# Indexer logits in two rounded passes a head, with the attention's first projection chunk between the heads

## The chip, the cores and the metric

The kernel runs on one core of a Trainium2 chip. The metric is the device time of one execution in microseconds. Before the change three runs took 1997.34, 1997.35 and 1994.6 us (median 1997.34).

## The reference

The reference is a stack of four layers on a sequence of 512 tokens with 1024 channels. The change touches the fourth mixer only, a sparse attention whose keys are chosen by an indexer. What it computes for a block of queries is

```python
logits = jnp.einsum('bqhd,bkd->bqhk', qi, k_idx_f)          # 8 index heads, 64 channels, one key for all heads
score = jnp.einsum('bqh,bqhk->bqk', wi, jax.nn.relu(logits))
score = jnp.where(s_pos[None, None, :] <= t_pos[None, :, None], score, -jnp.inf)
_, idx = lax.top_k(score, topk)                             # 128 keys per query
```

`qi`, `ki` and `wi` are columns of one projection of the normed input; other columns of the same projection are the queries, keys and values of the attention. A wrong order of two scores would choose another key, so the logits are wanted in nearly full precision.

## The kernel before

Every matrix product with weights is done in a rounded 32-bit format that TensorE streams faster than plain f32 (its type in the code is `F32R`). To keep precision each operand is split in a high part, which is the operand rounded, and a low part, which is the rest; the product is the sum of three: high by high, high weight by low activation, low weight by high activation (`three`). The activations are the tiles `h_hi` and `h_lo`. The weights come from HBM in chunks of 128x1024 by SyncE, and GpSimd splits them into `w_hi` and `w_lo`, four slots deep; it waits until the chunk four before is used up. A chunk (`tile_chunk`) is eight contraction tiles of three products of 512 columns, 24 products, into one of the four PSUM banks `gemm0` to `gemm3` (`G`). ScalarE copies the result out and so frees the bank.

The order on each engine is written out by hand, and engines wait on semaphores. Around the change it is this. Six chunks (`idx_in`) give the index queries (chunks 0 to 3, two heads of 64 rows each), the index key and the weights `wi` (chunk 4) and the latent rows (chunk 5). ScalarE copies them as plain f32 into tiles of `T2` (`b_t` in the profile); the key is copied twice, to rows 0 to 63 and 64 to 127, since both operands of a product must lie on the same rows. Then `index_logits(h)` runs for eight heads, L938: four products, one for each block of 128 queries, with 128, 256, 384 and 512 keys, as f32 with a contraction over the 64 rows of the head. The record of such a tile reads 64*128. Even heads write banks `G`, odd heads banks `M` (`mix` in the profile). After each head ScalarE evicts three pieces with Relu (L2063 to L2065), and VectorE adds them, weighted, to the score (L1595, L1597), four instructions a head. A head waits until the head two before is evicted. After head 0 four small transposes (L945) turn `wi`.

Behind the heads come eight one-column products for a norm (L953), which wait for the last eviction, then the attention's projection: four chunks, a broadcast of the norm's result (L557), four more chunks, and so on. The tiles go to `G` in the order of the chunks. Meanwhile VectorE takes the 128 largest scores of each query in sixteen rounds, then builds the biases, and meets TensorE again at the attention's logits (L1655).

## Time and profile before

| what | value |
|---|---|
| three runs, median | 1997.34 us |
| the profiled execution, its own time | 1993.52 us |
| its span from first to last instruction | 1991.7 us |
| mean granted TensorE clock | 0.986 |
| TensorE busy | 1926.6 us |
| weight loads | 1554.2 us |
| VectorE / ScalarE / GpSimd busy | 1033.4 / 452.7 / 1185.3 us |

Durations in the profile belong to this one execution. A busy TensorE is not a TensorE at its peak: the record of a product contains the time in the pipeline behind its last column, so that neighbours overlap, and what a product costs in a run is the time from its start to the next start. The granted clock stands as a share of 2.4 GHz: 1.00 is 2.4 GHz and 0.50 is 1.2 GHz. The type f32 is printed for rounded operands too, in the products.

### The profile page before, as it was taken

Reading aid. Unit: us, or ns where it says so; the run is one execution under the profiler, and the core shown is the slowest. Engines: PE = TensorE matmul, PEld = TensorE weight load, DVE = VectorE, ACT = ScalarE, POOL = GpSimd, SP = SyncE. Lnnn points to the kernel's source line nnn. Section 1 sums busy time; section 2 is a strip of 40 time slices with the busy share of each in tenths; the row PEclk is TensorE's granted clock in tenths of the full one; section 3 lists DMA queues with packets and bytes.
Section 4 is the critical chain, followed back from the end, with each engine's and each line's share of the span. In section 5 each row is a group of like instructions: output and inputs, shape, how many; then the busy total and the mean of one; then the engine's idle time right before and its main releaser. Section 6 shows DMA issues by size and latency. Waiting matters only on the chain.

```text
span 1991.7 us, 25332 instructions
## 1 busy us (share of the span) xinstructions
PE 1926.6 (97%) x8824; PEld 1554.2 (78%) x8824; DVE 1033.4 (52%) x1529; ACT 452.7 (23%) x774; POOL 1185.3 (60%) x907
## 2 busy tenths in 40 slices
PE   5999999999999999999999999999998899999998
PEld 4787868888888887667888888886776688888886
DVE  7566256666655453566766663334847453333222
ACT  3302342121110022342211121023118421111100
POOL 3743326788887956325687877743550256666773
PEclk7999999999999999999999999998999999999999
DMA  7532223555555422111455553322220023222332
GB/s 304 178 116 75 95 95 106 182 194 193 190 191 189 159 95 83 61 44 63 159 190 191 188 199 108 109 91 64 85 68 19 24 84 105 95 95 95 105 106 74
DMA packets 67375, 242.23 MB, mean 122 GB/s; under 512 B 7498, under 2 KB 7882, under 8 KB 67314
## 3 DMA queue, kind: packets, MB, share of 16 engines
q1 hardware_dynamic: 65536, 237.01, 34.4%
q10 hardware_dynamic: 1778, 4.37, 0.6%
q8 instruction: 43, 0.70, 0.2%
q14 instruction: 18, 0.15, 0.0%
HBM read 239.25 MB, written 2.10 MB: 121 GB/s over the span
## 4 chain that ended last, share of the span: by engine, by line
PE 89%; DVE 4%; ACT 3%; issue 2%; DMA 2%; POOL 1%; SPq 0%; ACTq 0%; DVEq 0%; POOLq 0%
PE gemm L446 24%; PE gemm L447 23%; PE gemm L448 23%; PE gemm L473 2%; PE gemm L475 2%; PE gemm L474 2%; DMA w_raw<-wstream 2%; PE mix L649 1%; PE gemm L802 1%; PE mix L446 1%; PE gemm L1036 1%; DVE sq_acc L1355 1%; PE mix L447 1%; PE mix L448 1%; PE gemm L816 1%
## 5 line engine op out<-in xcount | busy, mean ns | idle before, releaser
L430 POOL TENSOR_TENSOR w_lo<-w_raw,w_hi 128x1024 fp32r<-128x1024 f32 x302 | 735.7, 2436 | 25.2
L446 PE MATMUL gemm<-h_hi,w_hi 128*128 128x512 f32 x1616 | 634.4, 393 | 21.7 <-DVE h_lo L1176 14.9
L447 PE MATMUL gemm<-h_lo,w_hi 128*128 128x512 f32 x1616 | 631.0, 390 | 0.0
L448 PE MATMUL gemm<-h_hi,w_lo 128*128 128x512 f32 x1616 | 630.9, 390 | 0.0
L427 POOL TENSOR_TENSOR pool_gate<-pool_gate 128x1 f32<-128x1 f32 x298 | 118.3, 397 | 736.0 <-PE gemm L448 596.1
L446 PEld LDWEIGHTS gemm<-h_hi,w_hi 128*128 128x128 f32 x1616 | 304.7, 189 | 90.7 <-issue 22.6
L448 PEld LDWEIGHTS gemm<-h_hi,w_lo 128*128 128x128 f32 x1616 | 304.6, 188 | 63.8
L428 POOL TENSOR_SCALAR w_hi<-w_raw 128x1024 fp32r<-128x1024 f32 x302 | 344.2, 1140 | 16.9 <-DMA w_raw<-wstream 16.9
L447 PEld LDWEIGHTS gemm<-h_lo,w_hi 128*128 128x128 f32 x1616 | 304.7, 189 | 62.4
L1070 DVE CUSTOM_DVE_ANT_0 ada_raw<-ada_raw,c_act 128x1024 f32<-128x1024 f32 x128 | 218.3, 1722 | 108.4 <-DMA ada_raw<-adastream 108.4
L448 PE MATMUL gemm<-p_hi,w_lo 128*128 128x512 f32 x528 | 205.4, 389 | 0.0
L446 PE MATMUL gemm<-p_hi,w_hi 128*128 128x512 f32 x528 | 205.4, 389 | 0.0
L447 PE MATMUL gemm<-p_lo,w_hi 128*128 128x512 f32 x528 | 205.4, 389 | 0.0
L1088 DVE SCALAR_TENSOR_TENSOR x_res<-gemm,modv,x_res 128x512 f32<-128x512 f32 x48 | 35.9, 748 | 239.5 <-PE gemm L448 239.5
L1383 DVE TENSOR_TENSOR work<-work,gemm 128x512 f32<-128x512 f32 x66 | 45.4, 688 | 176.5 <-PE gemm L448 138.7
L1385 DVE TENSOR_TENSOR p_lo<-work,p_hi 128x512 f32 x66 | 97.5, 1477 | 61.4 <-ACT p_hi L1917 61.4
L1714 ACT ACTIVATE sq_tile<-x_res 128x512 f32 x48 | 30.4, 633 | 430.3 <-DVE x_res L1088 430.3
L1355 DVE TENSOR_TENSOR sq_acc<-sq_acc,sq_tile 128x512 f32<-128x512 f32 x42 | 98.8, 2353 | 36.7 <-ACT sq_tile L1714 36.7
L448 PEld LDWEIGHTS gemm<-p_hi,w_lo 128*128 128x128 f32 x528 | 99.1, 188 | 20.8
L446 PEld LDWEIGHTS gemm<-p_hi,w_hi 128*128 128x128 f32 x528 | 99.1, 188 | 20.6
L447 PEld LDWEIGHTS gemm<-p_lo,w_hi 128*128 128x128 f32 x528 | 99.1, 188 | 20.4
L1911 ACT ACTIVATE work<-work 128x512 f32<-128x512 f32 x44 | 27.9, 634 | 307.9 <-DVE work L1378 307.9
(341 smaller groups left out, 1970.4 us busy)
## 6 DMA issues: line engine op xcount, KB each, us to landing
w_raw<-wstream SPq DMA_DIRECT2D x302, 512.0 KB, 3.5
ada_raw<-adastream SPq DMA_DIRECT2D x128, 512.0 KB, 4.3
a_early<-adastream SPq DMA_DIRECT2D x8, 1024.0 KB, 11.8
out<-x_res SPq DMA_DIRECT2D x8, 256.0 KB, 2.2
c_act<-c_in ACTq DMA_DIRECT2D x2, 512.0 KB, 7.2
x_res<-x_in SPq DMA_DIRECT2D x2, 512.0 KB, 6.2
x_res<-x_in ACTq DMA_DIRECT2D x2, 512.0 KB, 9.1
b_dist<-const_in ACTq DMA_DIRECT2D x1, 512.0 KB
```

Of the source, the lines that this page charges most:

```text
L427: pool.tensor_tensor(pgate[:], pgate[:], pgate[:], ALU.mult)
L428: pool.tensor_scalar(whi[s][:], raw[:, u % RAW, :], 1.0, 0.0, ALU.mult, ALU.add).then_inc(w_hi_done, 1)
L430: pool.tensor_tensor(wlo[s][:], raw[:, u % RAW, :], whi[s][:].bitcast(F32), ALU.subtract).then_inc(w_split, 1)
L446: pe.matmul(out_ap, w_h, r_h, start=first, stop=False)
L447: pe.matmul(out_ap, w_h, r_l, start=False, stop=False)
L448: return pe.matmul(out_ap, w_l, r_h, start=False, stop=last)
L473: pe.matmul(G[j][:], a, wh, start=(k == 0), stop=False)
L474: pe.matmul(G[j][:], a, wl, start=False, stop=False)
L1070: dve.tensor_tensor_reduce(w, w, c, 1.0, start, ALU.mult, ALU.add, total).then_inc(ada_used, 1)
L1355: dve.tensor_tensor(sqacc[:], sqacc[:], sqt[:, m % 2, :], ALU.add).then_inc(sq_added, 1)
L1383: dve.tensor_tensor(work[:, 2 + jj, :], y, G[2 * jj + 1][:], ALU.mult).then_inc(gfree[2 * jj + 1], 1)
L1385: dve.tensor_tensor(Plo[:, ds(2 * i + jj, 1), :].rearrange("p a t -> p (a t)"), work[:, 2 + jj, :], Phi[:, ds(2 * i + jj, 1), :].rearrange ...
```

## The change

ScalarE now copies each index query tile five times: once as plain f32, and for each of its two heads the rounded value to rows 0 to 63 and to rows 64 to 127 of a tile of its own (`T2R`, the same memory as `T2` under the rounded type, `b_t_hilo` in the profile). VectorE subtracts the rounded value from the plain one, which gives the low part of the queries. The key tile `IDX_K2` gets the high part on rows 0 to 63 and the low part on rows 64 to 127, the tile `IDX_KD` the high part on both.

A block of logits is then two products in the rounded format. The first contracts over 128 rows: the high query, twice, against high and low key. The second contracts over the 64 rows of the head: the low query against the high key. The products of high by high, high by low and low by high are the same three as elsewhere.

The first chunk of the attention's projection no longer stands behind the norm's products. Its eight contraction tiles are done in pieces: two after head 1, and one after each of heads 2 to 7. It uses bank `G[3]`, which the heads don't use; the banks of the chunks behind it turn by one.

```diff
--- before.py
+++ after.py
@@ -288,6 +288,7 @@
             Z = [zmem[:, TRI * i:TRI * i + TRI] for i in range(3)] + [cact[:].rearrange("p m n -> p (m n)")[:, 0:TRI]]
             PS = sb("b_pt", [P, 2, TRI], F32, r)
             VB = work
+            IDX_Q, IDX_K2, IDX_KD = 6, 14, 15
             SB5 = M + [G[3]]
             rows = sqacc
             wuk = sb("b_wuk", [P, 4, P], F32, r)
@@ -301,6 +302,9 @@
             sm = sb("b_sm", [P, 16], F32, r)
 
 
+        with ExitStack() as r:
+            sb("r_over_h", [P, 2 * KT * T], F32, r)
+            T2R = sb("b_t2_hilo", [P, 18, T], F32R, r)
         const_in_sem = sem("const_loaded")
         x_loaded = [sem(f"x_loaded{m}") for m in range(4)]
         cols_loaded = sem("cols_loaded")
@@ -927,40 +931,60 @@
                 if h == 0:
                     for u in range(4):
                         pe.wait_ge(gfree[u], G0["attn_in"][u])
+                    pe.wait_ge(sig("ixk_low"), 1)
                 if h == 1:
                     pe.wait_ge(sig("wi_ready"), 1)
                     pe.wait_ge(sig("x_normed"), KT)
                 if h >= 2:
 
                     pe.wait_ge(sig("ix_relu"), h - 1)
+                pe.wait_ge(sig("ixq_low"), h + 1)
                 for j in range(NTB):
                     b, o = BANK_J[j]
-                    mm = pe.matmul(bk[b][:, o:o + P * (j + 1)], T2[rows, h // 2, j * P:(j + 1) * P], T2[rows, 4, 0:P * (j + 1)],
-                                   start=True, stop=True)
+                    n = P * (j + 1)
+                    pe.matmul(bk[b][:, o:o + n], T2R[:, IDX_Q + h, j * P:(j + 1) * P], T2R[:, IDX_K2, 0:n], start=True, stop=False)
+                    mm = pe.matmul(bk[b][:, o:o + n], T2R[rows, h // 2, j * P:(j + 1) * P], T2R[rows, IDX_KD, 0:n],
+                                   start=False, stop=True)
                 mm.then_inc(sig("ix_mm"), 1)
+
+            def first_query_chunk(ks):
+
+                n = N0["attn_in"]
+                s = n % SPL
+                for k in ks:
+                    if k == 0:
+                        pe.wait_ge(w_split, n + 1)
+                    mm = three(G[3][:], whi[s][:, k * P:(k + 1) * P], wlo[s][:, k * P:(k + 1) * P],
+                               Hhi[:, k, :], Hlo[:, k, :], k == 0, k == KT - 1)
+                if ks[-1] == KT - 1:
+                    mm.then_inc(pe_done, 1)
 
             index_logits(0)
 
             for j in range(NTB):
                 mm = pe.transpose(M[3][:, 8 * j:8 * j + 8], wirow[:, j * P:(j + 1) * P], const("ident")[0:8, 0:8])
             mm.then_inc(sig("wi_t"), 1)
-            for h in range(1, 8):
+            index_logits(1)
+            first_query_chunk((0, 1))
+            for h in range(2, 8):
                 index_logits(h)
+                first_query_chunk((h,))
 
             pe.wait_ge(sig("ckv_sq"), 1)
             pe.wait_ge(sig("ix_relu"), 8)
             for j in range(NTB):
                 mm = pe.matmul(normps[:, j:j + 1], sqt[:, 0, j * P:(j + 1) * P], const("ones")[:, 0:1], start=True, stop=True)
             mm.then_inc(norm_sum, 1)
-            def attn_tiles(first):
-
-                for u in range(4):
-                    tile_chunk(N0["attn_in"] + first + u, (N0["attn_in"] + u) % SPL, u, G0["attn_in"][u] + first // 4)
-
-            attn_tiles(0)
+            def attn_tiles(chunks):
+
+                for c in chunks:
+                    bank = (c + 3) % 4
+                    tile_chunk(N0["attn_in"] + c, (N0["attn_in"] + c) % SPL, bank, G0["attn_in"][bank] + c // 4)
+
+            attn_tiles(range(1, 4))
             bc[0] += 1
             bcast(rstdps, bc[0])
-            attn_tiles(4)
+            attn_tiles(range(4, 8))
 
             pe.wait_ge(sig("ckv_n"), 1)
             for u in range(4):
@@ -1576,7 +1600,19 @@
             ffn("ffn1", 1, COL["fconv_w"] + 66, 25, 21, C2, 11)
             down("down1", 4, 88, gain=True)
             norm(7, 6, col("g_attn", 0, 8), (96, 104), first_gain=col("final_g", 0, 8))
+            def index_lows(c):
+
+                for e in range(2):
+                    r = slice(64 * e, 64 * e + 64)
+                    dve.wait_ge(sig("ixq_high"), 2 * c + e + 1)
+                    dve.tensor_tensor(T2R[r, c, :], T2[r, c, :], T2R[r, IDX_Q + 2 * c + e, :].bitcast(F32),
+                                      ALU.subtract).then_inc(sig("ixq_low"), 1)
+
             normed_x(4, col("final_g", 0, 8), bank=M[1], done=True)
+            for c in range(4):
+                index_lows(c)
+            dve.wait_ge(sig("ixk_high"), 1)
+            dve.tensor_tensor(T2R[64:128, IDX_K2, :], T2[0:64, 4, :], T2R[0:64, IDX_K2, :].bitcast(F32), ALU.subtract).then_inc(sig("ixk_low"), 1)
 
             dve.wait_ge(small_loaded, 96)
 
@@ -2048,10 +2084,18 @@
                 if c == 4:
 
                     act.activation(T2[0:64, 4, :], G[0][0:64, :], ACT.Copy)
-                    act.activation(T2[64:128, 4, :], G[0][0:64, :], ACT.Copy)
+                    act.activation(T2R[0:64, IDX_K2, :], G[0][0:64, :], ACT.Copy).then_inc(sig("ixk_high"), 1)
+                    act.activation(T2R[0:64, IDX_KD, :], G[0][0:64, :], ACT.Copy)
+                    act.activation(T2R[64:128, IDX_KD, :], G[0][0:64, :], ACT.Copy)
                     act.activation(wirow, G[0][64:72, :], ACT.Copy, scale=IDX_SCALE).then_inc(gfree[0], 1)
+                elif c == 5:
+                    act.activation(T2[:, c, :], G[c % 4][:], ACT.Copy).then_inc(gfree[c % 4], 1)
                 else:
-                    act.activation(T2[:, c, :], G[c % 4][:], ACT.Copy).then_inc(gfree[c % 4], 1)
+                    act.activation(T2[:, c, :], G[c][:], ACT.Copy)
+                    act.activation(T2R[64:128, IDX_Q + 2 * c, :], G[c][0:64, :], ACT.Copy)
+                    act.activation(T2R[0:64, IDX_Q + 2 * c, :], G[c][0:64, :], ACT.Copy).then_inc(sig("ixq_high"), 1)
+                    act.activation(T2R[64:128, IDX_Q + 2 * c + 1, :], G[c][64:128, :], ACT.Copy).then_inc(sig("ixq_high"), 1)
+                    act.activation(T2R[0:64, IDX_Q + 2 * c + 1, :], G[c][64:128, :], ACT.Copy).then_inc(gfree[c], 1)
             act.activation(rms[:, 30:31], cols[:, 0:1], ACT.Copy).then_inc(sig("ckv_sq"), 1)
             act.wait_ge(sig("wi_t"), 1)
             act.activation(wi[:], M[3][:, 0:32], ACT.Copy).then_inc(sig("wi_ready"), 1)
@@ -2072,9 +2116,9 @@
                 act.activation(T2[:, tile, :], G[bank][:], ACT.Copy, scale=scale).then_inc(gfree[bank], 1)
 
             for u in range(4):
-                evict(u, u, 10 + u, 0.125)
+                evict(u, (u + 3) % 4, 10 + u, 0.125)
             for u in range(4):
-                evict(4 + u, u, 14 + u)
+                evict(4 + u, (u + 3) % 4, 14 + u)
             for u in range(4):
                 act.wait_ge(sig("kb_mm"), u + 1)
                 act.activation(T2[:, u, :], M[u][:], ACT.Copy).then_inc(sig("kb_copied"), 1)
```

TensorE, from the last product of the projection `idx_in` through head 0 and the transposes to the start of head 1. Before (`b_t` are the index tiles in f32; `gemm` and `mix` are the PSUM banks):

```order
L448 MATMUL gemm<-h_hi,w_lo 128x512
L938 MATMUL gemm<-b_t 128x128
L938 MATMUL gemm<-b_t 128x256
L938 MATMUL gemm<-b_t 128x384
L938 MATMUL gemm<-b_t 128x512
L945 MATMUL mix<-cst,b_pt 128x8 x4
L938 MATMUL mix<-b_t 128x128
```

After, in the same place, and on to the end of head 1, its six products of the chunk and the start of head 2 (L945 is now the product over 128 rows, L946 the one over 64):

```order
L945 MATMUL gemm<-b_t_hilo 128x384
L946 MATMUL gemm<-b_t_hilo 128x384
L945 MATMUL gemm<-b_t_hilo 128x512
L946 MATMUL gemm<-b_t_hilo 128x512
L965 MATMUL mix<-cst,b_pt 128x8 x4
L945 MATMUL mix<-b_t_hilo 128x128
L946 MATMUL mix<-b_t_hilo 128x128
```

```order
L945 MATMUL mix<-b_t_hilo 128x512
L946 MATMUL mix<-b_t_hilo 128x512
L450 MATMUL gemm<-h_hi,w_hi 128x512
L451 MATMUL gemm<-h_lo,w_hi 128x512
L452 MATMUL gemm<-h_hi,w_lo 128x512
L450 MATMUL gemm<-h_hi,w_hi 128x512
L451 MATMUL gemm<-h_lo,w_hi 128x512
L452 MATMUL gemm<-h_hi,w_lo 128x512
L945 MATMUL gemm<-b_t_hilo 128x128
L946 MATMUL gemm<-b_t_hilo 128x128
L945 MATMUL gemm<-b_t_hilo 128x256
```

Products over 128 and over 64 rows take turns within a head, and full products stand between heads.

ScalarE, the copies of the six projection chunks. Before:

```order
L2054 ACTIVATE b_t<-gemm 128x512 x4
L2050 ACTIVATE b_t<-gemm 64x512
L2051 ACTIVATE b_t<-gemm 64x512
L2052 ACTIVATE b_pt<-gemm 8x512
L2047 ACTIVATE sq_tile<-gemm 128x512
L2054 ACTIVATE b_t<-gemm 128x512
```

After, the fourth query tile, the key and the latent rows:

```order
L2097 ACTIVATE b_t_hilo<-gemm 64x512
L2098 ACTIVATE b_t_hilo<-gemm 64x512
L2086 ACTIVATE b_t<-gemm 64x512
L2087 ACTIVATE b_t_hilo<-gemm 64x512
L2088 ACTIVATE b_t_hilo<-gemm 64x512
L2089 ACTIVATE b_t_hilo<-gemm 64x512
L2090 ACTIVATE b_pt<-gemm 8x512
L2083 ACTIVATE sq_tile<-gemm 128x512
L2092 ACTIVATE b_t<-gemm 128x512
```

One copy of a query tile became five, and three of the key's chunk became five.

## Rows read from the trace of the kernel before

**Rows 1.** The page's header and TensorE's share of the span.
```profile
span 1991.7 us, 25332 instructions
PE 1926.6 (97%) x8824; PEld 1554.2 (78%) x8824; DVE 1033.4 (52%) x1529; ACT 452.7 (23%) x774; POOL 1185.3 (60%) x907
```

**Rows 2.** The chain of waits, 1330 to 1480 us: start, duration, what.
```profile
1364.96 1.36 issue
1366.33 2.39 PE gemm L938 x8
...
1385.11 0.60 ACT ada_raw L2063
...
1386.62 1.81 PE mix L953 x8
```

**Rows 3.** Time line of TensorE: start, duration, tile, shapes, count, idle before.
```profile
1368.65 0.41 PE L945 MATMUL mix<-cst,b_pt 8*128 8x8 f32 x4
1369.35 2.10 PE L938 MATMUL mix<-b_t 64*128 64x128 f32 x5 [0.29 <-ACT b_wi L2057]
...
1388.30 0.77 PE L446 MATMUL gemm<-h_hi,w_hi 128*128 128x512 f32 x1
...
1394.24 0.39 PE L446 MATMUL gemm<-h_hi,w_hi 128*128 128x512 f32 x1
...
1396.28 0.39 PE L446 MATMUL gemm<-h_hi,w_hi 128*128 128x512 f32 x1
```

**Rows 4.** Stretches: length, busy time (count) of each engine, clock, DMA share, GB/s.
```profile
1369.60:1372.90 3.30, 3.30 (x14) 2.76 (x14) 1.27 (x4) 0.95 (x3) 0.00 (x0) 0.50 0.49 159
1373.00:1386.60 13.60, 11.16 (x44) 6.35 (x43) 11.19 (x24) 9.43 (x21) 0.00 (x0) 1.00 0.00 0
1386.70:1393.40 6.70, 6.70 (x20) 5.64 (x21) 6.33 (x20) 0.27 (x1) 0.00 (x0) 0.50 0.00 0
1393.50:1412.00 18.50, 18.50 (x83) 15.29 (x82) 16.13 (x51) 1.80 (x3) 10.86 (x9) 1.00 0.17 57
```

**Rows 5.** Time line of TensorE: 40-row products between 128-row ones, clock 1.00.
```profile
822.02 0.50 PE L789 MATMUL mix<-o_gm_hilo,o_sel 40*128 40x512 f32 x1
822.45 0.50 PE L446 MATMUL mix<-h_hi,w_hi 128*128 128x512 f32 x1
...
914.75 0.40 PE L448 MATMUL gemm<-h_hi,w_lo 128*128 128x512 f32 x1
915.08 0.96 PE L850 MATMUL mix<-o_gm_hilo,o_sel 40*128 40x512 f32 x3
915.97 0.50 PE L446 MATMUL gemm<-h_hi,w_hi 128*128 128x512 f32 x1
916.31 0.39 PE L447 MATMUL gemm<-h_lo,w_hi 128*128 128x512 f32 x1
```

**Rows 6.** The same where the clock is 0.50.
```profile
807.79 0.79 PE L789 MATMUL mix<-o_gm_hilo,o_sel 40*128 40x512 f32 x1
808.51 0.79 PE L446 MATMUL mix<-h_hi,w_hi 128*128 128x512 f32 x1
809.10 0.63 PE L447 MATMUL mix<-h_lo,w_hi 128*128 128x512 f32 x1
```

**Rows 7.** Time line of ScalarE, copies of the index projection.
```profile
1348.68 0.60 ACT L2054 ACTIVATE b_t<-gemm 128x512 f32<-128x512 f32 x1 [5.77 <-PE gemm L448]
...
1365.00 0.60 ACT L2047 ACTIVATE sq_tile<-gemm 128x512 f32<-128x512 f32 x1 [3.64 <-PE gemm L448]
```

**Rows 8.** Time line of VectorE, scores and the start of the attention.
```profile
1370.68 1.27 DVE L1595 TENSOR_SCALAR b_score<-ada_raw,b_wi 128x128 f32<-128x128 f32 x4 [22.12 <-ACT ada_raw L2065]
1374.89 14.19 DVE L1597 SCALAR_TENSOR_TENSOR b_score<-ada_raw,b_wi,b_score 128x128 f32<-128x128 f32 x28 [2.93 <-ACT ada_raw L2065]
...
1413.69 0.69 DVE L1626 TENSOR_TENSOR b_t<-b_t,mix 128x512 f32<-128x512 f32 x1 [1.96 <-PE mix L557]
...
1468.76 0.29 DVE L1655 CUSTOM_DVE_ANT_0 ada_raw<-mix,b_bias 128x128 f32<-128x128 f32 x1 [9.38 <-PE mix L987]
```

## The prediction, on record before the result

> **What bounds the kernel now.** I first read the page's header and busy shares [rows 1]: TensorE is busy for 1926.6 of 1991.7 us. The chain of waits over the stretch of the change [rows 2] then shows what sets the end there. It runs almost wholly over TensorE: an idle 1.36 us (two evictions of the last projection chunk on ScalarE), the index logits, the evictions of the last head, eight one-column products, and the first chunk of the attention's projection. The time line of TensorE [rows 3] gives the stations: the heads begin at 1366.33, the one-column products at 1386.62, the first attention chunk at 1388.30, the second at 1396.28. So 29.95 us pass from the first logit to the second chunk, and the change has to be judged by what becomes of this stretch. The table of stretches [rows 4] adds the clock: 0.50 (1.2 GHz instead of 2.4) at 1369.6 to 1372.9 and again at 1386.7 to 1393.4. Last come the rows that show what a pass costs when its neighbours use another number of array rows [rows 5, 6].
>
> **The logits, passes alone.** A rounded 512-column product follows the next after 0.227 us (nine of them from 1394.24 to 1396.28 [rows 3]), one column a cycle at 2.4 GHz plus 0.014. A head has 128 + 256 + 384 + 512 = 1280 columns. In f32 they are the eight records of 1366.33, and the next instruction starts 2.32 us later [rows 2, 3]: four cycles a column, 2.13, and a tail. After there are two rounded passes a block: 2 x 1280 / 2400 = 1.07 us. Eight heads would win 8.5 us.
>
> **What the two passes add.** One pass contracts over 128 rows, the other over 64, and they alternate: eight changes of row count in a head (the order in the section on the change shows it). The trace has such changes of rounded products. One 40-row product of 512 columns between products of 128 rows: 822.02 to 822.45, so 0.43 us from start to start against the 0.23 of a run of equal ones [rows 5]. A run of three such products shows the parts: 0.33 into it (914.75 to 915.08), three of them until 915.97, and 0.34 instead of 0.23 from the first to the second after it. So the stop costs about 0.10 before the change and 0.11 for weights that are no longer loaded ahead: 0.21 on top of the stream for a pass that stands alone between two changes. The two head terms are then 8 x 0.21 + 1.07 = 2.75 us at 2.4 GHz: more than the 2.32 of before. At 1.2 GHz the 40-row product took 0.72 (807.79 to 808.51) and the second product behind it starts 0.59 after the first, where a run of equals has 0.43 [rows 6]: 0.29 a pass, so 2.13 + 8 x 0.29 = 4.5 us a head. The small blocks have no such row; I give them the same 0.21. Their bounds: nothing added (the second rival) and 0.21; I take 0.21, since the change came out the same wherever the trace has it.
> The Trainium skill (TensorEngine Tiling, section Key Properties) states that changing the tiling mode, unlike changing the tile within a mode, drains TensorE; by that rule, the trace agrees, with the 0.10 us above.
>
> **The chunk between the heads.** It moves 24 rounded products of 512 columns, 24 x 0.227 = 5.4 us, from behind the heads to between them. Before it took 7.98 us (1388.30 to 1396.28), because its first products ran at the low clock [rows 3, 4]: 2.5 us are lost there. A piece of three costs 0.68, plus 0.11 for its second weight load; the next head's first pass saves its 0.10.
>
> **The sum at the full clock.** Head 0: 1366.33 + 2.75 = 1369.1. Transposes and the copy of the weights, unchanged: 0.70 (1368.65 to 1369.35) [rows 3], so 1369.8. Head 1: 1372.5. Six products: 1.47, 1374.0. Six periods of 2.75 - 0.10 + 0.68 + 0.11 = 3.44: 1394.6. The one-column products wait for the evictions of head 7 (its passes end at 1393.8, evictions from 1385.11 to 1386.62 with the hand-over, 1.5 [rows 2]: 1395.3) and took 1.68 at the low clock (1386.62 to 1388.30 [rows 2, 3]), so 0.85 here: chunk two at 1396.2, against 1396.28. The passes' gain is spent on the changes, and the hidden chunk's on the longer heads. Nothing is left at this clock.
>
> **The clock.** It decides. It was down by 1369.6 in the trace: what stood before was the 1.36 us stop, 2.3 us of 64-row passes and the small transposes [rows 2 to 4]. It fell again behind the last head, with the 1.54 us wait. It came back by 1393.5, after five microseconds of full products without a gap (from 1388.30), and stayed [rows 4]. In the new kernel the first heads stand at the same place, behind the same stop, around the same transposes, and they stream 1.07 us in 2.75, half of it on 64 rows. So I expect the fall there too. The difference comes afterwards. Before, the next two heads' 64-row passes filled 1369.6 to 1372.9 without a gap (3.30 of 3.30 us busy), and the clock is back at 1373 [rows 4]. After, every head is stop and go, and between two heads stand only three products: 1.3 us, nothing like the unbroken run that brought the clock back. I let the loop run at 1.2 GHz to its end. Head 1: 1369.8 + 4.5 = 1374.3. Six products at 0.427 and one bare load of 0.17: 1377.0. Six periods of 4.5 + 1.28 = 5.8 (a load of 0.17 saved and one paid): 1411.7. Head 7 ends at 1410.4, evictions until 1411.9, the one-column products 1.7 (1386.62 to 1388.30, at this clock): 1413.6. The next chunk pays the way back to 2.4 GHz: before it was the 2.5 us; I take 1.9, since heads and pieces before it keep the engine busier than a wait did. That is 1415.5 against 1396.28: **+19.2 us**.
>
> **What hides the rest.** ScalarE gets 18 more activations (16 for four query tiles, two for the key), 0.60 us each. Eight of them follow the first two tiles, 4.8 us, where it then idles 5.77; two follow the key, 1.2 us, where it idles 3.64 [rows 7]. So 2.4 us of cover stand ahead of the last eviction, which frees the bank that head 0 waits for; what exceeded them would be added to the start. VectorE gets nine subtractions, and is idle for 22.12 us before the scores [rows 8], 2.5 us for each; the last one waits for the key's copy only, some four microseconds before head 0. The split weights of the attention's fifth chunk still wait for the end of its first, with three chunks (16 us) between them, so POOL's split and SP's transfer move along. VectorE's scores are 14.19 us for seven heads, 2.03 a head [rows 8], under the period of 3.44 or 5.8. But the last sum is now late: about 1413.9 instead of 1389.08, +24.9. The attention's first projection tiles arrive +19.2. VectorE has 9.38 us idle before the attention logits and 1.96 before the row of the norm, which goes since TensorE comes by one chunk earlier [rows 8]. 9.38 + 1.96 - 24.9 + 19.2 = 5.6 us are left, so VectorE does not set the end.
>
> **The time.** The profiled run took 1993.52, the three timed ones 1994.6 to 1997.35 with a median of 1997.34; their mean over all four is 1995.7. With +19.2 this gives 2014.9, told as 2015. By the profile alone it would be 2012.7, by the median 2016.5.
>
> **Rivals.**
> First, the clock holds, or comes back behind head 1 where six products stand together (2.6 us, with the wide passes around them). For it: the stretch 1373 to 1386.6 had waits of its own, 11.16 of 13.60 us busy, and held 1.00 [rows 4]; the pieces add full rows. Against it: head 0 and 1. It gives -0.1 if it never falls. If it falls for head 1 and the six, add 1.75 and 1.3, some +3 to +4. 1995.6 to 1999.7.
> Second, faster: the changes of row count cost nothing, since loads and drains overlap when both passes belong to one block. Then a head is 8 passes, 1.07 + 8 x 0.014 = 1.2 us, with its piece 1.9, and VectorE's 2.03 a head becomes the pace: head 1 ends at 1369.4, the six products at 1370.8, six times 2.03 to 1383.0, evictions and one-column products until 1385.3: -11 us, 1984.7. It decides once a pass costs less than 0.15 over its stream: 64 passes, 0.06 less each, are 4 us. For it: the small blocks and changes inside one block stand in no row. Against it: every change in rows 5 and 6 costs 0.2 and more.
> Third, the copies on ScalarE delay the start: at most a microsecond or two, by the cover above.
>
> **Chances.** Forecast 0.60, clock holds or returns 0.25, faster 0.13, worse than the forecast 0.02. A measurement of this kernel tells 0.2%, 4 us, from no change. So faster 0.13, same 0.25, slower 0.62. The range goes from the lower end of the first rival by the profiled run (1993.4) to the median plus 19.2 and a chunk wholly at the low clock (some +4): 1993 to 2020. The likeliest case alone: 2011 to 2019.
>
> **What would show it.** In the new profile: the 128-row and 64-row logit passes start 0.21 us apart beyond their stream (a 512-column pass 0.43); the clock reads 0.50 from about 1369 to 1415; the stretch from the first logit to the attention's second chunk is 49 us instead of 30; VectorE waits for ScalarE in the scores; its idle time before the attention logits shrinks to under 6 us. The forecast is wrong if the clock is 1.00 in the loop (then no change), or if passes follow each other at stream length (then faster).

## The result, and the profile after

The changed kernel is a little slower. Its median over 16 runs is 1998.88 us, against 1994.74 us over the same number of runs of the kernel before on the same chip (1990.49 to 1997.56): +4.1 us. The ratio is 1.0052, with a 95% interval of 1.0030 to 1.0073. It lies further above 1 than the two medians do (1.0021), since the 16 runs fall into two groups: nine at 1996.4 to 1999.1 us with a mean granted clock of 0.985 to 0.988, and seven at 2014.0 to 2018.5 us with 0.973 to 0.976. The profiled run, 2015.76 us, is of the upper group. All three profiles of this kernel are, so the rows here show that group alone.

The page's header and busy shares, as [rows 1]:
```profile
span 2014.0 us, 25365 instructions
PE 1950.7 (97%) x8824; PEld 1564.9 (78%) x8824; DVE 1050.0 (52%) x1538; ACT 462.8 (23%) x792; POOL 1186.1 (59%) x907
```
TensorE has exactly as many instructions as before, 8824: each head's four f32 products had two records each, and now it has eight rounded passes. It is busy for 24.1 us more.

The time line of TensorE, as [rows 3]: head 0 at the full clock, head 4 at the half clock, and the end of the loop.
```profile
1367.90 0.30 PE L945 MATMUL gemm<-b_t_hilo 128*128 128x128 f32 x1 [1.36 <-issue]
1368.13 0.32 PE L946 MATMUL gemm<-b_t_hilo 64*128 64x128 f32 x1
...
1369.76 0.50 PE L945 MATMUL gemm<-b_t_hilo 128*128 128x512 f32 x1
1370.19 0.50 PE L946 MATMUL gemm<-b_t_hilo 64*128 64x512 f32 x1
1370.62 0.41 PE L965 MATMUL mix<-cst,b_pt 8*128 8x8 f32 x4
...
1390.12 0.31 PE L945 MATMUL gemm<-b_t_hilo 128*128 128x128 f32 x1
...
1394.46 0.79 PE L450 MATMUL gemm<-h_hi,w_hi 128*128 128x512 f32 x1
...
1413.43 1.84 PE L976 MATMUL mix<-cst,sq_tile 128*128 128x1 f32 x8
1415.13 0.77 PE L450 MATMUL gemm<-h_hi,w_hi 128*128 128x512 f32 x1
...
1418.69 0.41 PE L452 MATMUL gemm<-h_hi,w_lo 128*128 128x512 f32 x1
```
Head 0 takes 1367.90 to 1370.62, 2.72 us; its 512-column passes stand 0.43 apart. A head at the half clock takes 1390.12 to 1394.46, 4.34 us (0.17 of a weight load stand in the piece around it). The second chunk starts at 1415.13, 47.2 us after the first logit, against 29.95 us before [rows 3].

The stretch of the loop, as [rows 4]: busy time (count) of TensorE, weight loads, VectorE, ScalarE, GpSimd, then the granted clock, the DMA share, GB/s.
```profile
1371.00:1418.60 47.60, 47.31 (x97) 27.59 (x97) 18.15 (x35) 11.74 (x27) 3.98 (x3) 0.50 0.03 11
```
The half clock covers 47.6 us without a break. Before, it covered twice, 3.3 and 6.7 us [rows 4].

The chain of waits (start, duration, what), as [rows 2]:
```profile
1382.96 0.72 PE gemm L450
...
1388.74 0.72 PE gemm L450
```
It stays on TensorE throughout; between the pieces L450, one behind each head, lie 5.78 us. The one-column products L976 no longer wait for ScalarE.

The time line of ScalarE, as [rows 7]:
```profile
1350.26 0.60 ACT L2094 ACTIVATE b_t<-gemm 128x512 f32<-128x512 f32 x1 [0.94 <-PE gemm L452]
...
1366.58 0.60 ACT L2083 ACTIVATE sq_tile<-gemm 128x512 f32<-128x512 f32 x1 [2.68 <-PE gemm L452]
```
That of VectorE, as [rows 8]:
```profile
1350.06 12.95 DVE L1608 TENSOR_TENSOR b_t_hilo<-b_t,b_t_hilo 64x512 fp32r<-64x512 f32 x8
1363.04 2.77 DVE L1615 TENSOR_TENSOR b_t_hilo<-b_t,b_t_hilo 64x512 fp32r<-64x512 f32 x1
...
1491.12 0.29 DVE L1691 CUSTOM_DVE_ANT_0 ada_raw<-mix,b_bias 128x128 f32<-128x128 f32 x1 [4.06 <-PE mix L1011]
```
ScalarE still idles 0.94 us after the first two tiles and 2.68 us after the key's copies. VectorE's nine subtractions end at 1365.8, two microseconds ahead of head 0. Before the attention logits VectorE idles 4.06 us, where it had 9.38.

Some of VectorE's instructions are longer than their equals. VectorE and GpSimd in two places of the same trace, the subtractions and the last head's sums:
```profile
1355.59 0.69 DVE L1608 TENSOR_TENSOR b_t_hilo<-b_t,b_t_hilo 64x512 fp32r<-64x512 f32 x1
...
1361.42 1.05 POOL L432 TENSOR_SCALAR w_hi<-w_raw 128x1024 fp32r<-128x1024 f32 x1
1361.43 1.57 DVE L1608 TENSOR_TENSOR b_t_hilo<-b_t,b_t_hilo 64x512 fp32r<-64x512 f32 x1
1362.55 2.71 POOL L434 TENSOR_TENSOR w_lo<-w_raw,w_hi 128x1024 fp32r<-128x1024 f32 x1
...
1413.70 1.27 POOL L432 TENSOR_SCALAR w_hi<-w_raw 128x1024 fp32r<-128x1024 f32 x1
1413.99 4.17 DVE L1633 SCALAR_TENSOR_TENSOR b_score<-ada_raw,b_wi,b_score 128x384 f32<-128x384 f32 x2
1415.06 2.56 POOL L434 TENSOR_TENSOR w_lo<-w_raw,w_hi 128x1024 fp32r<-128x1024 f32 x1
```
A subtraction takes 0.69 us with no split beside it, 1.57 beside GpSimd's L432 and 2.77 beside its L434, whose end (1365.26) it outlasts by half a microsecond. The last two sums, L1633, take 4.17 us for two, where before they took 1.27:
```profile
1387.81 1.27 DVE L1597 SCALAR_TENSOR_TENSOR b_score<-ada_raw,b_wi,b_score 128x384 f32<-128x384 f32 x2
```
Since the first attention chunk is now used up right behind head 7, GpSimd's next split starts at 1413.70 and falls on them; before, it started at 1396.68, 7.6 us behind their end.

The spans differ by 22.3 us. From head 0 to the first product of the attention's scores (at 1487.00 after and 1466.33 before; VectorE's L1691 waits for these products) 119.1 us pass instead of 100.0: +19.1. Head 0 starts 1.57 us later, since the clock fell once more early in that run (about 3.4 us at 190 us), and another short fall of the clock, at 1487.0, makes these products some 1.6 us longer.

### The profile page after: what moved, and what is told of

Same layout as the page of the kernel before. It is cut to its first block, busy times and chain, and to the rows that moved or that the text cites. A ratio compares the mean times of both kernels' runs of the same rounds, so it can differ in the third digit from the quotient of the medians.

```text
span 2014.0 us, 25365 instructions
## 1 busy us (share of the span) xinstructions
PE 1950.7 (97%) x8824; PEld 1564.9 (78%) x8824; DVE 1050.0 (52%) x1538; ACT 462.8 (23%) x792; POOL 1186.1 (59%) x907
## 4 chain that ended last, share of the span: by engine, by line
PE 89%; DVE 4%; ACT 3%; issue 2%; DMA 1%; POOL 1%; SPq 0%; ACTq 0%; DVEq 0%; POOLq 0%
PE gemm L450 23%; PE gemm L452 23%; PE gemm L451 23%; PE gemm L477 2%; PE gemm L479 2%; PE gemm L478 2%; DMA w_raw<-wstream 1%; PE mix L653 1%; PE gemm L806 1%; PE mix L450 1%; DVE sq_acc L1379 1%; PE gemm L1060 1%; PE mix L452 1%; PE mix L451 1%; PE gemm L820 1%
## 5 line engine op out<-in xcount | busy, mean ns | idle before, releaser
L434 POOL TENSOR_TENSOR w_lo<-w_raw,w_hi 128x1024 fp32r<-128x1024 f32 x302 | 735.7, 2436 | 25.2
L450 PE MATMUL gemm<-h_hi,w_hi 128*128 128x512 f32 x1616 | 637.0, 394 | 21.7 <-DVE h_lo L1200 14.9
L450 PEld LDWEIGHTS gemm<-h_hi,w_hi 128*128 128x128 f32 x1616 | 305.2, 189 | 93.3 <-issue 25.3
L432 POOL TENSOR_SCALAR w_hi<-w_raw 128x1024 fp32r<-128x1024 f32 x302 | 344.8, 1142 | 16.9 <-DMA w_raw<-wstream 16.9
L450 PE MATMUL gemm<-p_hi,w_hi 128*128 128x512 f32 x528 | 205.4, 389 | 0.0
L450 PEld LDWEIGHTS gemm<-p_hi,w_hi 128*128 128x128 f32 x528 | 99.1, 188 | 20.7
L451 PEld LDWEIGHTS gemm<-p_lo,w_hi 128*128 128x128 f32 x528 | 99.1, 188 | 20.5
L452 PEld LDWEIGHTS gemm<-p_hi,w_lo 128*128 128x128 f32 x528 | 99.1, 188 | 20.5
```

The source lines that it names most:

```text
L432: pool.tensor_scalar(whi[s][:], raw[:, u % RAW, :], 1.0, 0.0, ALU.mult, ALU.add).then_inc(w_hi_done, 1)
L434: pool.tensor_tensor(wlo[s][:], raw[:, u % RAW, :], whi[s][:].bitcast(F32), ALU.subtract).then_inc(w_split, 1)
L450: pe.matmul(out_ap, w_h, r_h, start=first, stop=False)
L451: pe.matmul(out_ap, w_h, r_l, start=False, stop=False)
L452: return pe.matmul(out_ap, w_l, r_h, start=False, stop=last)
```

## The experiments

Four theories stood against each other. A: a change between 128 and 64 rows costs 0.21 us, as in the prediction. B: every short pass costs that, whatever its neighbours. C: VectorE or ScalarE already sets the pace. D: the two groups are two courses of the clock, and it comes back, where it does, in the unbroken full products behind head 1. Kernels are compared with the kernel before on the same chip; "low" is the stretch at clock 0.50. The times in this table are from head 0's start to the start of the next whole chunk and to the first product of the attention's scores, each in one profile:

| kernel | low in the loop | to the next chunk | to the attention's scores |
|---|---|---|---|
| before | 3.4 and 6.8 us | 21.97 | 100.0 |
| the change | 47.8 us | 47.23 | 119.1 |
| grouped passes | 6.8 us | 24.22 | 94.4 |
| padded low pass | 3.4 us | 19.98 | 90.1 |
| logits only | 37.6 us | 37.99 | 115.2 |
| chunk only | 51.2 us | 49.01 | 121.5 |
| run of nine | 51.2 us | 48.51 | 121.4 |
| run of nine, second profile | 10.2 and 6.8 us | 35.51 | 107.9 |
| one piece each | 47.8 us | 46.65 | 118.9 |
| filled stops | none | 18.84 | 89.0 |

The next chunk is the attention's first in "before" and "logits only", its second in the others.

**Grouped passes.** The eight passes of a head are ordered so that the row count changes twice, not eight times. All products are the same.
```diff
-                for j in range(NTB):
+                wide = [(True, j) for j in (1, 2, 3)]
+                for full, j in wide + [(False, j) for j in (1, 2, 3, 0)] + [(True, 0)]:
```


> The changed kernel with the passes of a head in another order: wide passes of blocks 1, 2, 3, then the 64-row passes of 1, 2, 3, 0, then the wide pass of block 0. Two changes of row count in a head instead of eight, the same passes. Theory A (every change of row count costs a stop of 0.10 us and a bare weight load of 0.11): a head takes 1.07 + 0.11 + 2 x 0.21 = 1.6 us instead of 2.75, the period with its piece 2.3; about 9 us faster than before at the full clock, about 5 slower than before where the clock stays at 1.2 GHz through the loop, and that should be rarer than in the changed kernel, since the engine streams more of the time. Theory B (each short rounded pass costs 0.2 over its stream whatever stands beside it, because a 128-column weight load isn't hidden): a head still takes 2.75 us, and the time is that of the changed kernel.

Measured: 1989.20 us (1987.30 to 1991.28, six runs) against 1996.03; ratio 0.9966 (0.9954 to 0.9978), −6.8 us. Time line of TensorE:
```profile
1378.88 1.72 PE L948 MATMUL mix<-b_t_hilo 128*128 128x256 f32 x8
1380.43 0.45 PE L450 MATMUL gemm<-h_hi,w_hi 128*128 128x512 f32 x1
...
1381.19 1.72 PE L948 MATMUL gemm<-b_t_hilo 128*128 128x256 f32 x8
```
Its low stretch:
```profile
1371.10:1377.90 6.80, 6.80 (x19) 4.97 (x18) 3.22 (x8) 1.92 (x5) 0.00 (x0) 0.50 0.24 77
```
A head is 1.55 us (1378.88 to 1380.43) and the period 2.31. Against the 2.72 us of head 0 in the change, six changes fewer save 1.17, 0.20 each; against the 2.62 us of a head inside the loop (the run of nine, below) 1.07, 0.18 each. A holds. B, by which the order would change nothing, falls. The clock falls here too, behind the same stop, but it comes back after 6.8 us, behind the six products and near the end of head 2. All six runs lie within 4 us: no second group.

**Padded low pass.** The low query is multiplied over 128 rows as well. The second key tile exists twice, each with zeros on the rows of the other head, so that the product is the same and no row count changes.
```diff
-                    mm = pe.matmul(bk[b][:, o:o + n], T2R[rows, h // 2, j * P:(j + 1) * P], T2R[rows, IDX_KD, 0:n],
+                    mm = pe.matmul(bk[b][:, o:o + n], T2R[:, h // 2, j * P:(j + 1) * P], T2R[:, IDX_KD + h % 2, 0:n],
...
-                    act.activation(T2R[64:128, IDX_KD, :], G[0][0:64, :], ACT.Copy)
+                    act.activation(T2R[64:128, IDX_KD + 1, :], G[0][0:64, :], ACT.Copy)
+                    act.activation(T2R[64:128, IDX_KD, :], G[0][0:64, :], ACT.Copy, scale=0.0)
+                    act.activation(T2R[0:64, IDX_KD + 1, :], G[0][0:64, :], ACT.Copy, scale=0.0)
```


> The low-query pass also over 128 rows: the low parts of both heads of a tile against a key tile that holds the high key on the head's 64 rows and zeros on the other 64 (two such tiles, so two more copies on ScalarE). No change of row count anywhere in the loop but at the transposes. Theory A: a head takes 1.07 + 8 x 0.014 = 1.2 us, the period 1.9, and VectorE's 2.03 us a head becomes the pace; 11 us faster than before. Clock at 2.4 GHz behind head 1, since full rows stream nearly all the time. Theory B: as the changed kernel, 2.75 us a head. Theory C (VectorE or ScalarE pace the loop already): no gain over the changed kernel either, with TensorE idle between heads.

Measured: 1983.59 us (1982.41 to 1985.14, six runs); ratio 0.9939 (0.9927 to 0.9951), −12.4 us. No version of the study is faster. The time line of TensorE:
```profile
1371.78 0.22 PE L945 MATMUL gemm<-b_t_hilo 128*128 128x128 f32 x1
...
1372.59 0.39 PE L945 MATMUL gemm<-b_t_hilo 128*128 128x512 f32 x1
1372.82 0.40 PE L946 MATMUL gemm<-b_t_hilo 128*128 128x512 f32 x1
1373.06 0.40 PE L450 MATMUL gemm<-h_hi,w_hi 128*128 128x512 f32 x1
...
1373.75 0.22 PE L945 MATMUL mix<-b_t_hilo 128*128 128x128 f32 x1
...
1384.60 1.02 PE L976 MATMUL mix<-cst,sq_tile 128*128 128x1 f32 x8 [0.85 <-ACT ada_raw L2111]
```
The only stretch of its loop in which the clock is low:
```profile
1367.30:1370.60 3.30, 3.01 (x11) 2.68 (x11) 1.27 (x4) 1.66 (x5) 0.58 (x1) 0.50 0.44 135
```
Passes of 512 columns follow at 0.23 us, a head is 1.28 us and the period 1.97. As many passes, as short as in the change, now cost little more than their stream of 1.07 us: the price was the change of rows. C falls too, for the change: the period shrinks to 1.97 with VectorE's work as it was and two copies more on ScalarE. VectorE doesn't set this period, as the expectation had it: its last six heads take 14.97 us from 1374.65, 2.5 us each, and end 4.1 us behind the start of the next chunk (1385.48), and no eviction waits for them. The clock is low for 3.4 us.

**Logits only.** The two-pass logits of the change, with the attention's first chunk where it was before, behind the norm's products, and the banks in the old turn.
```diff
-            index_logits(1)
-            first_query_chunk((0, 1))
-            for h in range(2, 8):
+            for h in range(1, 8):
                 index_logits(h)
-                first_query_chunk((h,))
...
-            attn_tiles(range(1, 4))
+            attn_tiles(0)
```


> The two passes of logits, with the attention's first chunk where it was before, behind the heads. Theory A: 2.75 us a head at 2.4 GHz, so the second chunk starts 0.6 us later than in the kernel before, at 1.2 GHz 4.5 us a head and some 16 us later. Without full products between the heads the low clock should be the rule here: 14 to 18 us slower than before in most runs. Rival (it is the pieces between the heads that lose the time): no slower than before.

Measured: 2010.04 us (2009.45 to 2013.54, six runs); ratio 1.0076 (1.0063 to 1.0089), +14.0 us. The low stretch in the table of stretches:
```profile
1369.80:1407.20 37.40, 35.86 (x71) 19.81 (x71) 17.39 (x42) 10.51 (x24) 0.00 (x0) 0.50 0.03 13
```
With nothing but such heads the clock stays at 0.50 to their end and 3.4 us into the chunk behind them (which starts at 1365.89 + 37.99). All six runs have a mean clock of 0.977 to 0.980, so none came back early.

**Chunk only.** The f32 logits of before, without the copies and subtractions; only the chunk moves between the heads.
```diff
-                    n = P * (j + 1)
-                    pe.matmul(bk[b][:, o:o + n], T2R[:, IDX_Q + h, j * P:(j + 1) * P], T2R[:, IDX_K2, 0:n], start=True, stop=False)
-                    mm = pe.matmul(bk[b][:, o:o + n], T2R[rows, h // 2, j * P:(j + 1) * P], T2R[rows, IDX_KD, 0:n],
-                                   start=False, stop=True)
+                    mm = pe.matmul(bk[b][:, o:o + P * (j + 1)], T2[rows, h // 2, j * P:(j + 1) * P], T2[rows, 4, 0:P * (j + 1)],
+                                   start=True, stop=True)
```


> The f32 logits of before, with the attention's first chunk in pieces between the heads. Theory A: a head streams 2.13 us, two changes of row count and the piece bring the period to 3.1; 3 us faster than before if the clock holds at 2.4 GHz. If the clock falls in the loop as in the profiled run of the changed kernel, a period is about 6 us and the time 15 us over that of before. Rival (the chunk's first products at the low clock were the whole gain to be had, and it comes without the rounded logits): 2.5 us or more faster in every run.

Measured: 2016.49 us (2014.39 to 2021.13, five runs); ratio 1.0101 (1.0087 to 1.0115), +20.5 us. Time line of TensorE, head 1 and what follows:
```profile
1373.83 4.63 PE L938 MATMUL mix<-b_t 64*128 64x128 f32 x8 [0.29 <-ACT b_wi L2073]
1378.39 0.79 PE L446 MATMUL gemm<-h_hi,w_hi 128*128 128x512 f32 x1
```
The low stretch:
```profile
1373.60:1424.70 51.10, 50.87 (x100) 28.14 (x101) 19.36 (x39) 11.72 (x27) 3.98 (x3) 0.50 0.06 16
```
This one I had wrong on its cause. TensorE is busy for 50.87 of 51.10 us, the row count changes only twice a period, and yet the clock stays low in the profile, and by the mean clocks (0.973 to 0.977) in every run. So eight changes of row count a head, or TensorE standing still, are not needed for it to stay low. In the kernel before, the same f32 heads stand in the trace at clock 1.00 as well as at 0.50 [rows 4]. One thing that the pieces take from them can be seen there. Time line of TensorE before, heads 3 (`mix`) and 4 (`gemm`) and the start of head 5:
```profile
1374.91 1.56 PE L938 MATMUL mix<-b_t 64*128 64x128 f32 x6 [0.72 <-ACT ada_raw L2065]
1376.16 0.37 PE L938 MATMUL gemm<-b_t 64*128 64x128 f32 x1
...
1376.74 0.59 PE L938 MATMUL mix<-b_t 64*128 64x512 f32 x1
...
1378.78 1.99 PE L938 MATMUL mix<-b_t 64*128 64x128 f32 x7 [0.20 <-ACT ada_raw L2065]
```
Two f32 heads on different halves of the rows interleave: head 4 begins at 1376.16 while products of head 3 still come until 1376.74, and the two pass in 3.87 us, a wait of 0.20 included, where head 0 alone takes 2.32. With three full products between them each head stands alone, 4.56 us at the half clock. That is part of the loss; why the clock stays down is not explained. It also says that neither half of the change is good alone: +14.0 and +20.5, together +4 or +20.

**Run of nine.** For theory D: three pieces behind head 1 instead of two, then one after each of heads 2 to 6 and none behind head 7.
```diff
-            first_query_chunk((0, 1))
+            first_query_chunk((0, 1, 2))
             for h in range(2, 8):
                 index_logits(h)
-                first_query_chunk((h,))
+                if h < 7:
+                    first_query_chunk((h + 1,))
```


> The changed kernel with its pieces of the attention's first chunk placed otherwise: three contraction tiles (nine products) after head 1, one after each of heads 2 to 6, none after head 7. All instructions are the same. Theory D (the two groups of times of the changed kernel, about 1998 and about 2016, are two courses of the clock in the loop, and it comes back where a long enough run of full products stands behind head 1): the unbroken run at the low clock grows from 2.6 to 3.9 us, the clock comes back there in every run, and all runs lie near the lower group, 3 to 5 us over the kernel before. Rival (the two groups have another cause, for example the weights' transfers, or the place of the run plays no part): again two groups, or all in the upper one.

Measured: 2004.59 us in the median of six runs, ratio 1.0042 (1.0028 to 1.0055). The profiled one took 2016.26 at clock 0.975, the others 2002.39 to 2005.65 at 0.982 to 0.984. By these times and clocks five came back and one did not; and those that did cost +7 to +10 us, not the +3 to +5 expected. A second profile of it was taken:

> The kernel with nine products after head 1 and none after head 7, looked at once more, since its profile is of its one slow run (2016.26) and five others lie at 2002 to 2006. Theory D: in such a run the clock is back behind the nine products, and what it is above the lower group of the changed kernel (4 to 7 us) comes from the end of the loop: with no piece after head 7 TensorE waits 0.7 us longer for its evictions, and the clock falls there as it did in the kernel before, 2.5 us. Rival: the clock comes back later, behind another head.

It took 2007.58 us, and shows the course with the return. Time line of TensorE:
```profile
1386.67 0.22 PE L945 MATMUL mix<-b_t_hilo 128*128 128x128 f32 x1
...
1389.29 0.50 PE L450 MATMUL gemm<-h_hi,w_hi 128*128 128x512 f32 x1
...
1390.09 0.22 PE L945 MATMUL gemm<-b_t_hilo 128*128 128x128 f32 x1
...
1404.65 1.84 PE L977 MATMUL mix<-cst,sq_tile 128*128 128x1 f32 x8 [1.54 <-ACT ada_raw L2110]
```
The stretches:
```profile
1373.60:1383.70 10.10, 9.81 (x25) 6.28 (x24) 3.21 (x8) 2.81 (x7) 0.00 (x0) 0.50 0.15 52
1383.80:1404.20 20.40, 19.31 (x61) 10.77 (x61) 10.85 (x18) 7.87 (x18) 3.46 (x3) 1.00 0.00 0
1404.30:1411.00 6.70, 6.35 (x19) 5.41 (x20) 6.33 (x19) 0.96 (x3) 0.00 (x0) 0.50 0.24 81
```
The nine products run from 1378.94 to 1382.94 and the clock is 1.00 from 1383.76. From there a head is 2.62 us and the period 3.42 (1386.67 to 1390.09), the period that the prediction gave for the full clock. The second low stretch accounts for 3.4 us of what such a run costs: without a piece behind head 7 TensorE waits 1.54 us before the one-column products, as before [rows 2], and the clock falls again, for 6.8 us. In the profile that stayed low the same nine products stand from 1374.05 to 1378.06, 4.9 us behind the fall instead of 5.4, and the clock stays at 0.50 through them and until 1420.35:
```profile
1369.20:1420.30 51.10, 49.27 (x102) 29.40 (x102) 22.23 (x48) 11.74 (x27) 3.96 (x3) 0.50 0.07 21
```
The instructions up to the fall are the same in both, but the fall comes 3.0 us behind the start of head 0 here (1366.14), as in the three profiles of the change, and 2.7 us behind it (1370.84) in the profile with the return. Whether that decides the course, one profile with a return can't tell.

**One piece each.** The other way: piece 0 behind the transposes, before head 1, and one behind each of heads 1 to 7, so that nowhere more than three products stand together.
```diff
-            index_logits(1)
-            first_query_chunk((0, 1))
-            for h in range(2, 8):
+            first_query_chunk((0,))
+            for h in range(1, 8):
```


> The changed kernel with one contraction tile after each of the eight heads, so that no run longer than three products stands in the loop. The first stands behind the transposes, in TensorE's wait before head 1. Theory D: once the clock is down it has nowhere to come back; all runs, or nearly all, in the upper group, 18 to 20 us over the kernel before, unless the piece in the wait keeps it from falling at all. Rival (run length plays no part): two groups in the same shares as in the changed kernel, 0.7 us earlier.

Measured: 2015.10 us (2013.75 to 2018.03, four runs), ratio 1.0103 (1.0087 to 1.0118). The low stretch:
```profile
1369.40:1417.10 47.70, 47.70 (x98) 27.64 (x97) 18.90 (x38) 11.54 (x26) 3.98 (x3) 0.50 0.05 14
```
No run came back: all four are in the upper group, with mean clocks of 0.974 to 0.976, though the piece before head 1 leaves TensorE no stop in the low stretch. With the later profiles the change stays out of the upper group in nine of 18 runs, and the run of nine in six of seven. So the clock was spared or returned in none of four, nine of 18 and six of seven runs, in the order of the run's length. That fits D as a matter of frequency, not as the rule that I had expected. It is not proven: the runs are few, the change can't be told apart from either neighbour by them, the two versions also differ in what stands before head 1 and behind head 7, and a return is seen in one profile alone.

**The change again.** Two more profiles of the changed kernel, to catch one of its lower group.

> The changed kernel itself, looked at once more, since its one profile is of the upper group of its times (2015.76). Theory D: a run of the lower group (near 1998) has the clock back at 2.4 GHz right behind the six products of head 1, or not lost in the loop at all; the periods of heads 2 to 7 are then 3.44 us, head 2 begins about 3 us later than at the full clock, and the second chunk begins 3 to 4 us later from head 0 than before. A run of the upper group repeats the first profile.

> As the look before: one more chance for a profile of the lower group, with the same expectations.

2015.69 and 2014.04 us: both in the upper group again, with the low stretch as long to a tenth (47.8 us). There is no profile of the lower group.

**Filled stops.** The padded version, with pieces where TensorE stood still: two in the stop before head 0, one behind the transposes, none behind heads 1 and 7.
```diff
+            pe.wait_ge(gfree[3], G0["attn_in"][3])
+            first_query_chunk((0, 1))
             index_logits(0)
...
+            first_query_chunk((2,))
             for h in range(1, 8):
```


> The kernel with the padded key tiles (no change of row count in the loop), with two contraction tiles of the attention's chunk in the 1.36 us stop before head 0, one in the wait behind the transposes, none after head 1, and one after each of heads 2 to 6. The loop is paced by VectorE at 2.03 us a head from head 1 on, and starts it at the same point; head 2 comes 1.4 us earlier and head 7's evictions about 1 us earlier: 1 to 1.5 us faster than the padded kernel, and the clock doesn't fall at head 0 any more, 0.5 us more. Rival (the loop's end is set by TensorE's own work, which is only moved): 2 us faster, the length of the stops filled. Rival (the chain is that of ScalarE and VectorE alone): the same time as the padded kernel.

Measured: 1985.89 us (1983.24 to 1987.29, five runs), ratio 0.9952 (0.9938 to 0.9965). Time line of TensorE:
```profile
1367.77 0.30 PE L945 MATMUL gemm<-b_t_hilo 128*128 128x128 f32 x1
...
1385.73 1.02 PE L979 MATMUL mix<-cst,sq_tile 128*128 128x1 f32 x8 [2.80 <-ACT ada_raw L2114]
```
ScalarE's waits for VectorE in the loop (us in total, times, longest):
```profile
ACT ada_raw L2112 <- DVE b_score L1636: 4.3, 5, 1.5
```
The stretch in which all its heads lie:
```profile
1366.00:1390.00 24.00, 21.19 (x117) 17.90 (x116) 17.42 (x32) 12.95 (x30) 8.10 (x6) 1.00 0.21 66
```
In this profile the clock never falls in the loop. So the fall of the padded version, 3.4 us, hangs on the stops around the first heads, 1.36 us before head 0 and 0.29 before head 1, which are filled here. The second alone is not it: the one piece each fills that one too, and its clock falls. For the kernels with changes of row count the filled stops were not tried. But the stop comes back at the end: TensorE waits 2.80 us for the last evictions, where the padded version waits 0.85. The evictions of heads 3 to 7 wait for VectorE's sums, 4.3 us together, so here VectorE does set the pace, as expected. From head 0 to the next chunk it gains 1.14 us, in the total nothing that can be told: 9.2 us under its own runs of before, 12.4 for the padded version.

## Why the prediction was right and where it was wrong

The sign was right, and the measured median lies in the range. The forecast of 2015 us was right for seven runs of 16, wrong for the median. That the range holds it is owed to the first rival, from which its lower end comes; the likeliest case alone, 2011 to 2019, misses it. And +4.1 us is not a size that the mechanism gave: it depends on how many of the 16 runs fell in each group.

**What failed is a step of the part on the clock: "I let the loop run at 1.2 GHz to its end."** I took this as the course of every run and gave it 0.60. In nine of 16 runs the mean clock is about 0.986, not 0.975. What that means can be checked in size: at 0.975 of 2014 us the lost share is 2 x 0.025 x 2014 = 101 us at the half clock; at 0.986 of 1996 it is 56 us. The 45 us between them are nearly the low stretch of 47.8 us. So in these runs the clock is not low through the loop, and at +1.6 to +4.4 us over the median of before they are my first rival (+3 to +4, chance 0.25). Whether it comes back early or doesn't fall there at all the mean clocks can't tell: a step of 0.001 in them is 4 us at the half clock. That it comes back at the six products is inferred: from the run of nine, where a trace shows it behind nine, and from the one piece each, where no run returned. Which of the two courses a run takes is open. The instructions are the same; the two profiles of the run of nine differ ahead of their nine products in the moment of the fall (3.0 and 2.7 us behind the start of head 0), and two profiles don't settle it.

**The terms, where the clock was as forecast.** A head at the full clock: 2.75 us told, 2.72 and 2.62 measured. A period at the full clock 3.44, measured 3.42; at the half clock 5.8, measured 5.78. From first logit to the end of the one-column products 47.3 us (1413.6 less 1366.33), measured 47.23; the 49 us among the signs are the same with the way back to the full clock added. The way back, told as 1.9: the next chunk's first eight products take 3.56 us from start to start (1415.13 to 1418.69), where eight at 0.227 are 1.8, so 1.7. Head 0 to the attention's scores: +19.2 told, +19.1 measured.

**The change of row count.** 0.21 us for each lone pass was taken from 40-row products [rows 5]. On 64 rows it is 0.43 from start to start for 512 columns, 0.23 for 128 (0.053 streamed), so 0.18 to 0.22: the small blocks, which stood in no row, cost the same. Grouping and padding show that it is the change of row count that costs, and not the length of a pass. The second rival (changes cost nothing, −11 us) named what the kernel would be without it: 1.2 us a head, 2 us a period. The padded version is that kernel, 1.28 and 1.97, −12.4 us. What the f32 heads cost was read too high: 2.32 us is a head alone, and at the full clock two of them pass in 3.87 us (heads 3 and 4, shown with the chunk only), 1.94 each. So the passes had no 8.5 us to win on heads of 2.13 us and a tail. The sum was not hurt by it, since it was held against the measured end of the loop.

**What hides the rest.** ScalarE's cover of 2.4 us held: its idle time of 5.77 before the third tile shrank to 0.94, by the 4.8 told, and that of 3.64 to 2.68. VectorE's subtractions were under 2.5 us on average, as allowed (12.95 us for eight), but more than twice the 0.69 us of one with no split beside it, and the last one ended 2.1 us before head 0, not four. The slack before the attention logits was 4.06 us instead of 5.6. There the prediction let GpSimd's split "move along" and did not look at what it moves onto: the last head's sums, which became 2.9 us longer (4.17 less 1.27). The sums ended 50.3 us behind the first logit, and 47.6 were told. The other 1.2 us, which came the other way, I did not separate. None of it reached the end, since the slack covered it. The Trainium skill (SBUF — State Buffer, section "SBUF: two separate sides") states that VectorE and GpSimd arbitrate for one pair of ports, which one instruction holds for its whole length while the other waits, where VectorE's instruction has two inputs in SBUF. The trace agrees: 0.69 us with no split beside it, and beside one 1.57 and 2.77 us, ending about half a microsecond behind the split each time.

## What to carry to other kernels

A rounded product is priced by its start-to-start distance beside the neighbours that it will have: two short passes with another row count each can cost more than the f32 product that they replace, above all where f32 products on different halves of the rows interleave. Zero rows that keep the count the same, or passes grouped by row count, took this from +4 to −12.4 and −6.8 us. Where a stretch begins behind a stop of TensorE, work out both courses of the clock, give neither all the weight, and time enough runs to see whether there are two groups.

## What the runs showed of the hardware

- The same program took two courses of the clock on one chip, with medians 18 us apart, nine to seven in 16 runs, with nothing between 1999.2 and 2013.9 us.
- TensorE was busy for 50.87 of 51.10 us and was granted 0.50 throughout, where f32 heads on 64 rows made up three quarters of the time (4.56 of a period of 6.14) and three full products the rest. All five runs of it were 18 us or more above the median of the kernel before.
- With every pass on 128 rows the clock was back after 3.4 us, TensorE being busy for 3.01 of 3.30 us; in the kernel before it was back as soon with f32 passes on 64 rows, 3.30 of 3.30 us busy [rows 4].
- Two f32 heads on different halves of the rows passed in 3.87 us, where one alone took 2.32.
- A rounded pass of 512 columns took 0.23 us beside passes of the same row count and 0.43 where the row count changed before and behind it; 128 columns took 0.23 there.
- The same 64x512 subtraction of VectorE took 0.69, 1.57 or 2.77 us, by what GpSimd did beside it.
